# Delta rule mixer: projections in the order k, q, z, v, blocks sent ahead of a tile's wait, values solved and read out by halves of the heads

## The chip, the cores and the metric

The kernel runs on one core of one Trainium2 chip. The metric is the device time of one launch in microseconds (us), as the median of several runs. Engines: PE is TensorE (matmul), PEld its weight load, DVE VectorE, ACT ScalarE, SP the engine that issues the DMAs. GpSimd has nothing to do here.

## The reference, cut to what matters

The whole program is a chain of two stacks on an activation of 256 tokens x 1024. The first stack has two layers: a SwiGLU, a mixer, cross attention, a SwiGLU. The second has four layers of other mixers and MLPs. Everything is float32. The change touches one mixer, that of the second layer of the first stack, `deltanet_mixer`:

```python
qkv, z, a, b = jnp.split(h @ w_in, [3 * W, 4 * W, 4 * W + DN_HEADS], axis=-1)   # W = 1024, 8 heads of 128
qkv = jax.nn.silu(causal_dwconv(qkv, conv_w))                                  # 4 taps
q, k, v = jnp.split(qkv, 3, axis=-1)
q, k = l2norm(q), l2norm(k)
beta = sigmoid(b); g = -exp(a_log) * softplus(a + dt_bias)
# per head and chunk:
decay = exp(where(tril, gcum_i - gcum_j, -inf))
amat = eye + where(strict, (k*beta) k^T * decay, 0)
sol = triangular_solve(amat, [v*beta, k*beta*exp(gcum)], lower, unit_diagonal)  # u and w
qk = q k^T * decay
v_new = u - w @ state;  o = (q*exp(g)) @ state + qk @ v_new
state = state*exp(g_last) + (k*exp(g_last - g))^T @ v_new
o = rmsnorm(o, o_norm) * silu(z)
return o @ w_out
```

The result is added to the activation, and cross attention follows, whose keys and values are projections of another input, `mem`, that doesn't depend on the mixer.

## The kernel before, in words

**Weights.** All weight matrices lie in DRAM as 836 tiles of 128 x 1024 float32 (512 KB). Each is used once. For tile t, SP issues its DMA into one of three buffers SL (L2643) once VectorE has split tile t-3. ScalarE copies it to WH in a rounded format (`hi`, L1888), VectorE subtracts, WL = SL - WH (`lo`, L890), and TensorE multiplies with both halves. There are four buffers of WH and of WL: `hi(t)` waits until TensorE is through with tile t-4. A tile is four *blocks* of 128 x 256, and a block is six matmuls (two halves of the columns, each WH with the high part of the activation, WH with its low part, WL with the high part). `walk` on ScalarE and VectorE issues `hi` and `lo` of the tile three ahead at the start of each tile, then the engine's other work of that tile in the order of the code. So whatever stands ahead of a `hi` or a `lo` in its engine's stream delays it, and what waits for something slow delays all tiles after it.

**The stage.** The four projections of the mixer are the tiles 258 to 289, that is 128 blocks, numbered x = 0 to 127 in the order dn.k, dn.z, dn.q, dn.v (32 each, a group of 256 output columns every 8). After them come four small stages whose weights do not depend on the mixer: xv1a and xv1b (values for cross attention, 4 tiles each, 8 steps k of two blocks), xk1a and xk1b (its keys, 4 tiles each, 16 blocks), and then the mixer's output projection dn.o. The mixer's own arithmetic runs *beside* these blocks. Each engine has a function `beside(x)` that lists by block number what is to be issued ahead of block x. Nothing is scheduled at run time: the block numbers are the schedule, and each engine runs its stream in order.

**What runs beside** (TensorE's part in small float32 matmuls into three PSUM banks, taken in turn by `small`: the fourth use waits until the first was read):
- `taken(g)`, `taps(g)`, `conv(g)`, `gate(g)`: group g of k (0 to 3), q (4 to 7) or v (8 to 11) is evacuated on VectorE, its last tap is set on ScalarE, three taps are added on VectorE (six instructions), and SiLU is taken on ScalarE, for k and q with the squares.
- `squares(j)`: sums of squares over a head on TensorE; `spread` evacuates them. `log_sd` and `exp_sd` (ScalarE) turn four of them into the inverse norm, and `normalize` (VectorE) applies it. `log_sd` begins with a load of an activation table.
- `masked`, `exp_decay`: the decay matrices DC and its transpose DT, from the cumulated gates; `dkk`: k k^T per head, times DC; `dlt` its transpose.
- The 16 x 16 blocks on the diagonal of that matrix go through DRAM (`blocks_of_16` on SP) into a layout in which VectorE inverts them all at once (`eliminate`, 15 steps of two instructions), and back in two times eight DMAs into Y and YT.
- `invert`: three levels that double the size of the inverted blocks. In a level TensorE first makes four products dm, then four pairs dy and dyt; VectorE masks or subtracts each.
- `dkq`: k q^T, times DT; `dkt` and `keys`: k turned and scaled; `dvt` and `values`: v turned and scaled; `duu` and `dwt`: the solved values and keys; `dkv`: the state after the first chunk; `dws` with `less_state`; `do`: the output (`read_out`), evacuated by `output`. A number behind a name is a quarter q: two of a head's chunks times four heads; quarters 0 and 1 are the first chunk of the heads 0 to 3 and 4 to 7, 2 and 3 the second.
- `head_sums`, `sd_of`, `inverse_root`, `finish`, `finished`: the norm of the output, times silu(z), split into high and low parts for dn.o.

Of the kernel before, what the change touches and what calls it, by code (L numbers as in the profile page):

```python
# [49 lines left out]
def stage_table():  # L50
    rows = []
    for layer in range(2):
        rows += [(f"f1.{layer}.in", 8, 22, 1), (f"f1.{layer}.out", 22, 4, 1)]
        if layer == 0:
            rows += [("ab.q", 8, 2, 1), ("ab.k", 8, 2, 1), ("ab.x", 8, 2, 1), ("ab.v", 8, 1, 2), ("xk0", 8, 4, 1),
                     ("ab.g", 8, 2, 1), ("xv0", 8, 2, 2), ("ab.o", 8, 4, 1)]
        else:
            rows += [("dn.k", 8, 4, 1), ("dn.z", 8, 4, 1), ("dn.q", 8, 4, 1), ("dn.v", 8, 4, 1), ("xv1a", 8, 1, 2), ("xv1b", 8, 1, 2), ("xk1a", 8, 2, 1),
                     ("xk1b", 8, 2, 1), ("dn.o", 8, 4, 1)]
# [50 lines left out]
def build_program(nc, w, pk, cp, xT_in, mem_in, pos_in, out):  # L110
# [13 lines left out]
    with ctx:  # L124
# [90 lines left out]
        SUMMED = (33, 35, 37, 41, 84, 92, 100, 108)  # L215
# [42 lines left out]
        def tensor_program(p):  # L258
# [232 lines left out]
            def deltanet():  # L491
# [61 lines left out]
                def beside(x):  # L553
# [9 lines left out]
                    if 50 <= x < 54:  # L563
                        p.wait_ge(dn_qk.sem, dn_qk["k"])
                        four(("dkk", x - 50), lambda i: part(2048, 4 * (x - 50) + i), lambda i: part(2048, 4 * (x - 50) + i))
                    if 55 <= x < 59:
                        freed(("dkk", x - 55))
                        turned(("dlt", x - 55), lambda i: sl(L, x - 55, i))
                    if 88 <= x < 112:
                        invert((x - 88) // 8, (x - 88) % 8)  # L570
                    if 113 <= x < 117:
                        turned(("dkt", x - 113), lambda i: part(2048, 4 * (x - 113) + i))
                    if 122 <= x < 126:
                        p.wait_ge(dn_qk.sem, dn_qk["q"])
                        four(("dkq", x - 122), lambda i: part(2048, 4 * (x - 122) + i), lambda i: part(0, 4 * (x - 122) + i))
# [39 lines left out]
                for name in ("dn.k", "dn.z", "dn.q", "dn.v"):  # L615
# [3 lines left out]
                for j, k in gemm("xv1a", R67, R67, 0, 2048):  # L619
                    if k % 2 == 0:  # L620
                        p.wait_ge(mp_lo.sem, mp_lo[1, k // 2])
                    if k < 2:
                        solve_keys(2 + k)
                    if 3 <= k < 7:
                        q = (0, 2, 1, 3)[k - 3]
                        p.wait_ge(dn_act.sem, dn_act[9 + 2 * (q % 2)])
                        turned(("dvt", q), lambda i: part(4096, 4 * q + i))
                    if k == 5:
                        solve_values(0)
                    if k == 7:  # L630
                        solve_values(1)
                for j, k in gemm("xv1b", R67, R67, 0, 2048):
                    if k in (0, 1):
                        solve_values(2 + k)
                        add_keys(k)
                    if k in (2, 3):
                        read_out(k - 2)
                        less_state(k)
                    if k in (5, 6):
                        read_out(k - 3)  # L640
                for j, k in gemm("xk1a", R67, R67, 0, 2048):
                    if j == 0 and 1 <= k < 5:
                        head_sums(k - 1)
# [242 lines left out]
        def vector_program(v):  # L886
# [353 lines left out]
            def deltanet(gain):  # L1240
# [131 lines left out]
                def beside(x):  # L1372
# [15 lines left out]
                    if x in (24, 32) or x % 8 == 0 and x > 71:  # L1388
                        taken(x // 8 - (1 if x < 64 else 5))
                    if x in (25, 33) or x % 8 == 2 and x > 71:  # L1390
                        conv(x // 8 - (1 if x < 64 else 5))
# [4 lines left out]
                    if x in (35, 37, 40, 43):  # L1396
                        masked((35, 37, 40, 43).index(x))
                    if x % 8 == 7 and 32 <= x < 64:
                        scaled_to("dn.z", x // 8 - 4, BIG, 6144)
                    if x == 47:  # L1400
                        normalize("k", BIG[:, 2048:4096], PG[3], 1.0)
                    if 51 <= x < 55:
                        q = x - 51
# [4 lines left out]
                    if 66 <= x < 74:  # L1408
                        eliminate(2 * x - 132)
                        if x < 73:  # L1410
                            eliminate(2 * x - 131)
                    if x == 74:
                        own()
                        v.tensor_copy(TT, T.rearrange("p r c -> p c r")).then_inc(dn_sub.sem, dn_sub.give("t"))
                    if x == 87:
                        v.wait_ge(dn_exp.sem, dn_exp["er"])
                        v.tensor_copy(KE.unsqueeze(2), q4(DT)[:, :, 127:128]).then_inc(V.sem, V.up())
                    if 89 <= x < 113:
                        invert((x - 89) // 8, (x - 89) % 8)
                    if 114 <= x < 118:  # L1420
                        if x == 114:
                            own()
                            v.wait_ge(dn_beg.sem, dn_beg["g"])
                        keys(x - 114)
                    if x == 119:
                        normalize("q", BIG[:, 0:2048], PG[3], 128.0 ** -0.5)
                    if 123 <= x < 127:
                        q = x - 123
                        bk, free = had(("dkq", q))
                        v.tensor_tensor(QT[:, hc(q)], bk[:, :], DT[:, hc(q)], ALU.mult).then_inc(free, 1)  # L1430
                    if x == 127:
                        taken(11)
                        v.tensor_tensor(Q3, Q3, q4(ER[:, 1024:2048]), ALU.mult).then_inc(dn_qg.sem, dn_qg.give("qg"))
                    if x in (124, 126):
                        mem_low(x - 124)
                        mem_low(x - 123)
                for x in range(2):
                    v.memset(xp[x][:, :, 0:3], 0.0).then_inc(V.sem, V.up())
                x = 0
                for name in ("dn.k", "dn.z", "dn.q", "dn.v"):  # L1440
# [3 lines left out]
                for c in range(4, 8):  # L1444
                    mem_low(c)
# [1380 lines left out]
```

## Time and profile before

| | us |
|---|---|
| runs: median (lowest to highest of 3) | 2885.52 (2877.37 to 2886.12) |
| the profiled execution: device time | 2886.11 |
| its span in the trace | 2884.3 |
| PE busy | 2724.6 (94%) |
| DVE busy | 1819.3 (63%) |
| ACT busy | 1410.9 (49%) |
| mean granted clock of TensorE | 0.975 of full |

The span begins with the first instruction and ends with the last; the execution's own time is 1.8 us longer. Engines run beside each other, so busy times don't add up. A row of idle time gives in brackets how long an engine stood before the instruction and what released it. The granted clock is the share of full speed (2.4 GHz) that the throttle gave TensorE, 0.50 being 1.2 GHz.

### The profile page before, as it was taken

To read this page: it belongs to the slowest core of one execution; us is meant where nothing else is said; L and a number is where in the kernel's file an instruction comes from. 1 tells how busy PE (TensorE), PEld (TensorE's weight loads), DVE (VectorE), ACT (ScalarE), POOL (GpSimd) and SP (SyncE) were. 2 spreads that over 40 slices of the span, in tenths; PEclk is the share of its full clock that TensorE was granted. 3 is DMA by queue.
4 is the path that set the end of the run, shared out by engine and by line. 5 is a ranking of instruction groups with operands and counts; after the bars stand their busy time and mean duration, and the time that the engine had idled before them with its cause. 6 is when DMAs were issued, how large, how long until landed. Compare 5 with 4: busy or idle time off the path is not lost. (4 is left out here: it accounts for less than half of the span.)

```text
span 2884.3 us, 48970 instructions
## 1 busy us (share of the span) xinstructions
PE 2724.6 (94%) x21046; PEld 2631.0 (91%) x21046; DVE 1819.3 (63%) x2346; ACT 1410.9 (49%) x1924; POOL 0.2 (0%) x4
## 2 busy tenths in 40 slices
PE   7998989999998898999999999979999899999998
PEld 7998889999997878999888999979988899889998
DVE  5657656656656646666655765877554785655764
ACT  5445545454456354544445455544455544445443
POOL 0000000000000000000000000000000000000000
PEclk9999999999999999999999999999999999999999
DMA  6553435555543124455444455325542465444463
GB/s 211 176 190 126 162 109 194 183 190 184 189 146 114 59 96 146 162 187 190 159 153 134 154 198 162 109 66 191 193 154 95 143 198 190 152 163 137 154 196 128
DMA packets 129000, 450.09 MB, mean 156 GB/s; under 512 B 20112, under 2 KB 20368, under 8 KB 128528
## 3 DMA queue, kind: packets, MB, share of 16 engines
q1 hardware_dynamic: 128784, 446.96, 47.2%
q8 instruction: 166, 2.72, 0.4%
q14 instruction: 50, 0.41, 0.0%
HBM read 445.47 MB, written 1.44 MB: 155 GB/s over the span
## 5 line engine op out<-in xcount | busy, mean ns | idle before, releaser
L260 PE MATMUL B<-R,WH 128*128 128x256 f32 x10432 | 2105.4, 284 | 61.9 <-DVE R L956 37.1
L260 PEld LDWEIGHTS B<-R,WH 128*128 128x128 f32 x10432 | 1695.1, 191 | 76.6 <-DVE R L956 27.5
L890 DVE TENSOR_TENSOR WL<-SL,WH 128x1024 fp32r<-128x1024 f32 x836 | 1011.3, 1223 | 796.4 <-ACT WH L1888 795.4
L260 PE MATMUL B<-R,WL 128*128 128x256 f32 x4480 | 1267.1, 283 | 0.0
L1888 ACT ACTIVATE WH<-SL 128x1024 fp32r<-128x1024 f32 x836 | 866.4, 1053 | 576.3 <-PE B L260 475.8
L260 PEld LDWEIGHTS B<-R,WL 128*128 128x128 f32 x4480 | 857.3, 191 | 0.0
L260 PE MATMUL B<-RB,WH 128*128 128x256 f32 x1984 | 556.4, 280 | 0.0
L260 PE MATMUL B<-RB,WL 128*128 128x256 f32 x1728 | 482.5, 279 | 0.0
L260 PEld LDWEIGHTS B<-RB,WH 128*128 128x128 f32 x1984 | 373.6, 188 | 0.4 <-DVE WL L890 0.2
L260 PEld LDWEIGHTS B<-RB,WL 128*128 128x128 f32 x1728 | 324.0, 187 | 0.0
L260 PE MATMUL B<-WH,R 128*128 128x512 f32 x480 | 159.6, 402 | 3.1 <-DVE WL L890 3.0
L260 PE MATMUL B<-PG 128*128 128x256 f32 (+6 forms) x672 | 134.9, 349 | 12.1 <-DVE PG L1345 4.3
L260 PEld LDWEIGHTS B<-PG 128*128 128x128 f32 (+2 forms) x672 | 111.7, 197 | 27.6 <-issue 7.3
L1956 ACT ACTIVATE R<-X,PK 128x256 fp32r<-128x256 f32 x128 | 61.3, 505 | 118.5 <-DVE X L964 66.4
L2363 ACT ACTIVATE RB<-PG 128x512 fp32r<-128x512 f32 x64 | 40.5, 633 | 159.6 <-DVE PG L1484 159.6
L260 PEld LDWEIGHTS B<-WH,R 128*128 128x128 f32 x480 | 90.6, 189 | 28.8 <-DVE WL L890 5.2
L260 PE MATMUL B<-WL,R 128*128 128x512 f32 x240 | 95.2, 397 | 0.0
L260 PE MATMUL B<-PG,ONES 128*128 128x256 f32 (+1 forms) x242 | 71.6, 417 | 23.8 <-DVE PG L931 8.6
L2053 ACT ACTIVATE RB<-PG 128x512 fp32r<-128x512 f32 x44 | 27.8, 632 | 130.2 <-DVE PG L1048 130.2
L956 DVE SCALAR_TENSOR_TENSOR R<-X,PK,R 128x256 fp32r<-128x256 f32 x128 | 59.0, 483 | 29.1 <-ACT R L1956 29.1
L979 DVE TENSOR_TENSOR R<-PG,RB 128x512 fp32r<-128x512 f32 x108 | 73.9, 684 | 3.3 <-ACT RB L2053 2.8
L2050 ACT ACTIVATE PG<-PG 128x512 f32<-128x512 f32 x44 | 27.9, 633 | 91.7 <-DVE PG L1041 91.7
(280 smaller groups left out, 1522.5 us busy)
## 6 DMA issues: line engine op xcount, KB each, us to landing
SL<-in_w SPq DMA_DIRECT2D x836, 512.0 KB, 3.5
CP<-in_cp SPq DMA_DIRECT2D x5, 768.0 KB, 4.9
X<-in_xT SPq DMA_DIRECT2D x2, 512.0 KB, 6.6
PG<-in_mem SPq DMA_DIRECT2D x1, 1024.0 KB, 10.8
out<-X SPq DMA_DIRECT2D x1, 1024.0 KB, 3.9
PK<-in_pk SPq DMA_DIRECT2D x1, 594.5 KB, 3.8
dn_y<-PG SPq DMA_DIRECT2D x1, 256.0 KB, 4.1
PG<-dn_y SPq DMA_DIRECT2D x16, 16.0 KB, 2.0
```

Of the source, the lines that this page charges most:

```text
L260: return p.matmul(o, left, right, start=first, stop=final, skip_group_check=True)
L890: v.tensor_tensor(WL[t % NSPL][:, :], SL[t % NRAW][:, :], WH[t % NSPL][:, :].bitcast(F32), ALU.subtract).then_inc(s_lo, 1)
L956: v.scalar_tensor_tensor(R67[:, 2048 + c * 256:2304 + c * 256], X[:, cc(c)], gain(c), R67[:, cc(c)].bitcast(F32), ALU.mult, ALU.subtract). ...
L979: v.tensor_tensor(R03[:, hc(u)], d, RB[:, hc(u)].bitcast(F32), ALU.subtract).then_inc(hid_lo.sem, hid_lo.give((f, u)))
L1888: a.activation(WH[t % NSPL][:, :], SL[t % NRAW][:, :], ACT.Copy).then_inc(s_hi, 1)
L1956: a.activation(R67[:, cc(c)], X[:, cc(c)], ACT.Copy, scale=gain(c)).then_inc(h_hi.sem, h_hi.give((n, c)))
L2050: a.activation(s, s, ACT.Silu).then_inc(silu.sem, silu.give((f, u)))
L2053: a.activation(RB[:, hc(u)], PG[10][:, u % 4 * 512:u % 4 * 512 + 512], ACT.Copy).then_inc(hid_hi.sem, hid_hi.give((f, u)))
L2363: a.activation(RB[:, hc(x)], PG[10][:, x % 4 * 512:x % 4 * 512 + 512], ACT.Copy).then_inc(hid_hi.sem, hid_hi.give((f, x)))
```

## The change

Four things are changed, all in the schedule; no instruction's arithmetic is.

1. The projections run in the order k, q, z, v, and the weights are laid out in that order. So q's groups are convolved beside blocks 40 to 65, where z's groups were only evacuated, and `dkq` moves from block 122 to 84.
2. On SP, the DMAs of `blocks_of_16` stand ahead of the wait for the split of tile t-3, one tile number later.
3. The block numbers of the rest are moved to suit: `normalize("k")` from 47 to 50, `dkk` from 50 to 53, `eliminate` from 66 to 70, `invert` from 88 to 92, z's evacuation from 39 to 71 and on.
4. Behind the projections, quarters 0 and 2 (heads 0 to 3) are turned, solved and read out first, then 1 and 3, and the norm of the output follows earlier.

The core of the diff (of the table of weights and of what is only renumbered, a line or two):

```diff
-            rows += [("dn.k", 8, 4, 1), ("dn.z", 8, 4, 1), ("dn.q", 8, 4, 1), ("dn.v", 8, 4, 1), ...
+            rows += [("dn.k", 8, 4, 1), ("dn.q", 8, 4, 1), ("dn.z", 8, 4, 1), ("dn.v", 8, 4, 1), ...
-        SUMMED = (33, 35, 37, 41, 84, 92, 100, 108)
+        SUMMED = (24, 27, 38, 43, 57, 59, 66, 75)
 # TensorE
-                    if 50 <= x < 54:
+                    if 53 <= x < 57:                      # dkk
-                    if 55 <= x < 59:
+                    if x in (58, 60, 61, 62):             # dlt
+                    if 84 <= x < 88:                      # dkq, was 122 <= x < 126
-                    if 88 <= x < 112:
+                    if 92 <= x < 116:                     # invert
+                    if 116 <= x < 120:                    # dkt, was 113
+                    if x in (122, 124):
+                        solve_keys(x // 2 - 59)
+                    if x in (125, 127):
+                        turn_values(x - 125)
 # TensorE, xv1a
-                    if k < 2:
-                        solve_keys(2 + k)
...
+                    if k in (0, 2):
+                        solve_values(k)
+                    if k == 3:
+                        add_keys(0)
+                    if k in (4, 5):
+                        turn_values(2 * k - 7)
                     if k == 5:
-                        solve_values(0)
+                        less_state(2)
+                    if k == 6:
+                        solve_values(1)
+                        read_out(0)
                     if k == 7:
-                        solve_values(1)
+                        solve_values(3)
 # VectorE
+                    if x % 8 == 0 and (16 < x < 72 or x > 96):
+                        taken(x // 8 - (1 if x < 72 else 5))
+                    if x % 8 == (1 if x < 72 else 2) and (20 < x < 72 or x > 99):
+                        conv(x // 8 - (1 if x < 72 else 5))
-                    if x in (35, 37, 40, 43):
+                    if x in (35, 37, 67, 69):             # masked
-                    if x % 8 == 7 and 32 <= x < 64:
+                    if x % 8 == 7 and 64 <= x < 96:       # evacuation of z
-                    if x == 47:
+                    if x == 50:
                         normalize("k", BIG[:, 2048:4096], PG[3], 1.0)
-                    if 66 <= x < 74:
+                    if 70 <= x < 78:                      # eliminate
+                    if x == 82:
+                        normalize("q", BIG[:, 0:2048], PG[3], 128.0 ** -0.5)
+                    if x == 126:
+                        values(0)
 # VectorE, xv1a and xk1a
+                    if k == 0:
+                        conv(11)
+                        values(2)
+                    if k == 5:
+                        values(1)
+                    if k == 6:
+                        less_state(2)
+                        values(3)
-                    if j == 1 and k in (1, 5):
-                        finish(k // 2)
+                    if j == 0 and k in (4, 7):
+                        finish(k // 7 * 2)
 # ScalarE
-                    if x in (17, 22, 30, 37, 79, 87, 95, 102, 110, 118, 126):
+                    if x in (17, 22, 34, 38, 52, 53, 61, 70, 109, 117, 126):   # gate
-                    if x in (43, 111):
-                        log_sd(x // 111)
+                    if x in (45, 77):
+                        log_sd(x // 77)
-                        exp_decay("dc", DC, GC2, x - 46)
+                        exp_decay("dc", DC, GC2, x - 47)
+                    if 79 <= x < 83:
+                        exp_decay("dt", DT, NGC, x - 79)
-                    if (j, k) in ((0, 6), (1, 0)):
-                        finish(2 * j)
+                    if j == 0 and k in (1, 3):
+                        finish(k - 1)
 # SP
-                if t == T0 + 20:
+                if t == T0 + 21:                          # and each of the others one later
+                blocks_of_16(t)
                 if t >= NRAW:
                     s.wait_ge(s_lo, t - NRAW + 1)
-                blocks_of_16(t)
                 s.dma_start(SL[t % NRAW][:, :], w[t]).then_inc(s_w[t % NRAW], 16)
```

Where the change moves instructions, at three places. First VectorE around `normalize("k")` (the SCALAR_TENSOR_TENSOR of 128x2048), ahead of which TensorE waits for `dkk`. L890 is the split of a weight tile, L1263 `taken`, L1275 `conv`, L983 the evacuation of z, L1310 `masked` for DT, L1407 the product with DC. Before:

```order
L890 TENSOR_TENSOR WL<-SL,WH 128x1024
L1310 TENSOR_TENSOR PG<-CP,PG 128x1024 x2
L890 TENSOR_TENSOR WL<-SL,WH 128x1024
L983 TENSOR_TENSOR BIG<-B,RST 128x512
L1298 SCALAR_TENSOR_TENSOR BIG<-BIG,PG 128x2048
L890 TENSOR_TENSOR WL<-SL,WH 128x1024
L1407 TENSOR_TENSOR H<-B,PG 128x512
```

After (L906 is the split, L1279 `taken`, L1291 `conv`, L1314 `normalize`, L1423 the product with DC):

```order
L906 TENSOR_TENSOR WL<-SL,WH 128x1024
L1279 TENSOR_TENSOR PG<-B,RST 128x2x256
L1291 SCALAR_TENSOR_TENSOR BIG<-PG,PK,BIG 128x256 x6
L906 TENSOR_TENSOR WL<-SL,WH 128x1024 x2
L1279 TENSOR_TENSOR PG<-B,RST 128x2x256
L1291 SCALAR_TENSOR_TENSOR BIG<-PG,PK,BIG 128x256 x6
L1314 SCALAR_TENSOR_TENSOR BIG<-BIG,PG 128x2048
L906 TENSOR_TENSOR WL<-SL,WH 128x1024
L1423 TENSOR_TENSOR H<-B,PG 128x512 x2
```

The fourth and fifth groups (q's first two) are now evacuated and convolved ahead of the normalization of k, and so are two more splits.

Next ScalarE at the same place. Before: L1888 is `hi`, L2208 `spread`, L2214 and L2218 `log_sd` and `exp_sd`, L2224 `exp_decay`:

```order
L1888 ACTIVATE WH<-SL 128x1024
L2208 ACTIVATE PG<-B 128x512
L1924 ACT_TABLE_LOAD
L2214 ACTIVATE PG<-PG,PK 128x2048
L1888 ACTIVATE WH<-SL 128x1024
L2218 ACTIVATE PG<-PG 128x2048
L2275 ACTIVATE RT<-RT 128x16
L2277 ACTIVATE RT<-RT 128x16
L2224 ACTIVATE PG<-PG,RT 128x128 x8
L1888 ACTIVATE WH<-SL 128x1024
```

After: L1917 is `hi`, L2221 `taps`, L2237 `spread`, L2243 and L2247 `log_sd` and `exp_sd`, L2253 `exp_decay`:

```order
L1917 ACTIVATE WH<-SL 128x1024
L2221 ACTIVATE BIG<-PG,PK 128x256 x2
L1917 ACTIVATE WH<-SL 128x1024
L2237 ACTIVATE PG<-B 128x512
L1953 ACT_TABLE_LOAD
L2243 ACTIVATE PG<-PG,PK 128x2048
L2247 ACTIVATE PG<-PG 128x2048
L2313 ACTIVATE RT<-RT 128x16
L2315 ACTIVATE RT<-RT 128x16
L2253 ACTIVATE PG<-PG,RT 128x128 x4
L1917 ACTIVATE WH<-SL 128x1024
L2221 ACTIVATE BIG<-PG,PK 128x256 x2
L2253 ACTIVATE PG<-PG,RT 128x128 x12
```

The two `taps` of q came in, the `hi` between logarithm and exponential went, and a `hi` with a quarter of the decay matrix now stands between the exponential and the rest.

Last, VectorE in xk1a, where the output of the mixer is scaled (L1460, after L1489) and split into its low part (L1071, after L1087), four quarters in two calls of `finish`. Before:

```order
L1238 TENSOR_TENSOR BIG<-BIG 128x512 x4
L890 TENSOR_TENSOR WL<-SL,WH 128x1024 x2
L1460 SCALAR_TENSOR_TENSOR BIG<-BIG,PK,PG 128x256 x2
L1071 TENSOR_TENSOR R<-BIG,R 128x512
L1460 SCALAR_TENSOR_TENSOR BIG<-BIG,PK,PG 128x256 x2
L1071 TENSOR_TENSOR R<-BIG,R 128x512
L890 TENSOR_TENSOR WL<-SL,WH 128x1024
L1460 SCALAR_TENSOR_TENSOR BIG<-BIG,PK,PG 128x256 x2
L1071 TENSOR_TENSOR R<-BIG,R 128x512
L1460 SCALAR_TENSOR_TENSOR BIG<-BIG,PK,PG 128x256 x2
L1071 TENSOR_TENSOR R<-BIG,R 128x512
L890 TENSOR_TENSOR WL<-SL,WH 128x1024 x6
```

After:

```order
L906 TENSOR_TENSOR WL<-SL,WH 128x1024
L1254 TENSOR_TENSOR BIG<-BIG 128x512 x2
L906 TENSOR_TENSOR WL<-SL,WH 128x1024
L1489 SCALAR_TENSOR_TENSOR BIG<-BIG,PK,PG 128x256 x2
L1087 TENSOR_TENSOR R<-BIG,R 128x512
L1489 SCALAR_TENSOR_TENSOR BIG<-BIG,PK,PG 128x256 x2
L1087 TENSOR_TENSOR R<-BIG,R 128x512
L1489 SCALAR_TENSOR_TENSOR BIG<-BIG,PK,PG 128x256 x2
L1087 TENSOR_TENSOR R<-BIG,R 128x512
L1489 SCALAR_TENSOR_TENSOR BIG<-BIG,PK,PG 128x256 x2
L1087 TENSOR_TENSOR R<-BIG,R 128x512
L906 TENSOR_TENSOR WL<-SL,WH 128x1024 x8
```

Of the three splits ahead of and between the two calls of `finish`, two now stand behind both.

## Rows read from the trace of the kernel before

**Rows 1.** By window: PE, PEld, DVE, ACT, POOL busy us, clock, DMA, GB/s

```profile
845.00:926.00 81.00, 64.45 (x476) 60.01 (x475) 53.53 (x98) 55.65 (x96) 0.00 (x0) 0.92 0.35 107
926.00:988.00 62.00, 54.33 (x408) 51.99 (x409) 34.75 (x58) 15.56 (x21) 0.00 (x0) 0.92 0.23 70
988.00:1012.00 24.00, 19.48 (x155) 18.84 (x154) 21.10 (x34) 11.88 (x16) 0.00 (x0) 0.93 0.27 89
1012.00:1057.00 45.00, 39.53 (x233) 33.92 (x232) 19.39 (x27) 20.21 (x33) 0.00 (x0) 0.96 0.26 88
1057.00:1088.00 31.00, 28.21 (x205) 26.09 (x204) 17.40 (x24) 20.84 (x28) 0.00 (x0) 0.94 0.34 111
```

**Rows 2.** Timeline of TensorE, rows after a wait: start, us, work, [idle before, releaser]

```profile
853.75 1.13 PE L260 MATMUL B<-CP,PG 128*128 128x128 f32 x8 [1.62 <-ACT RT L2263]
...
879.68 1.65 PE L260 MATMUL B<-BIG 128*128 128x128 f32 x6 [2.73 <-DVE BIG L1298]
...
916.44 2.05 PE L260 MATMUL B<-PG,ONES 128*128 128x512 f32 x2 [5.80 <-ACT PG L2204]
...
926.01 1.25 PE L260 MATMUL B<-PG 128*128 128x128 f32 x8 [3.93 <-issue]
...
950.41 0.85 PE L260 MATMUL B<-PG 128*128 128x128 f32 x4 [2.16 <-DVE PG L1345]
...
1083.14 0.51 PE L260 MATMUL B<-R,WH 128*128 128x256 f32 x2 [2.79 <-DVE WL L890]
```

**Rows 3.** By window: the clock after a short and a longer wait

```profile
937.30:941.30 4.00, 3.99 (x35) 4.00 (x36) 1.52 (x3) 0.00 (x0) 0.00 (x0) 1.00 0.43 135
951.00:954.00 3.00, 3.00 (x16) 3.00 (x15) 3.00 (x8) 0.00 (x0) 0.00 (x0) 0.50 0.23 90
```

**Rows 4.** Timeline of VectorE: the pace of tiles, undisturbed

```profile
816.53 1.23 DVE L890 TENSOR_TENSOR WL<-SL,WH 128x1024 fp32r<-128x1024 f32 x1 [1.60 <-ACT WH L1888]
819.36 1.23 DVE L890 TENSOR_TENSOR WL<-SL,WH 128x1024 fp32r<-128x1024 f32 x1 [1.60 <-ACT WH L1888]
```

**Rows 5.** Timeline of TensorE: two groups of four products, a block between

```profile
882.71 1.05 PE L260 MATMUL B<-BIG 128*128 128x128 f32 x8
...
884.31 0.94 PE L260 MATMUL B<-BIG 128*128 128x128 f32 x7
```

**Rows 6.** Timeline of ScalarE around log_sd

```profile
870.63 0.60 ACT L2208 ACTIVATE PG<-B 128x512 f32<-128x512 f32 x1 [0.45 <-PE B L260]
871.25 1.28 ACT L1924 ACT_TABLE_LOAD   x1
872.55 2.01 ACT L2214 ACTIVATE PG<-PG,PK 128x2048 f32<-128x2048 f32 x1
...
875.40 1.90 ACT L2218 ACTIVATE PG<-PG 128x2048 f32<-128x2048 f32 x1
...
877.42 2.43 ACT L2224 ACTIVATE PG<-PG,RT 128x128 f32<-128x128 f32 x8
```

**Rows 7.** Timeline of VectorE: taken, conv, normalize

```profile
860.52 0.68 DVE L1263 TENSOR_TENSOR PG<-B,RST 128x512 f32<-128x512 f32 x1
862.25 2.47 DVE L1275 SCALAR_TENSOR_TENSOR BIG<-PG,PK,BIG 128x256 f32<-128x256 f32 x6 [1.04 <-ACT BIG L2192]
...
877.34 2.29 DVE L1298 SCALAR_TENSOR_TENSOR BIG<-BIG,PG 128x2048 f32<-128x2048 f32 x1
```

**Rows 8.** Groups of VectorE, 901 to 913 us: the elimination

```profile
L1329 DVE TENSOR_TENSOR PG<-PG 128x15 f32<-128x15 f32 (+7 forms) x15 | 3.1, 208 | 0.5
```

**Rows 9.** Timeline of SP: the blocks on their way through DRAM

```profile
916.41 0.33 SPq L2624 DMA_DIRECT2D dn_y<-PG  x1
...
920.54 3.86 SPq L2629 DMA_DIRECT2D PG<-dn_y  x8
```

**Rows 10.** Timeline of VectorE: finish, one quarter and the next

```profile
1070.34 0.87 DVE L1460 SCALAR_TENSOR_TENSOR BIG<-BIG,PK,PG 128x256 f32<-128x256 f32 x2
...
1072.52 0.88 DVE L1460 SCALAR_TENSOR_TENSOR BIG<-BIG,PK,PG 128x256 f32<-128x256 f32 x2
```

More of the change, by code:

```diff
@@ L57, in stage_table @@
         else:
-            rows += [("dn.k", 8, 4, 1), ("dn.z", 8, 4, 1), ("dn.q", 8, 4, 1), ("dn.v", 8, 4, 1), ("xv1a", 8, 1, 2), ("xv1b", 8, 1, 2), ("xk1a", 8, 2, 1),
+            rows += [("dn.k", 8, 4, 1), ("dn.q", 8, 4, 1), ("dn.z", 8, 4, 1), ("dn.v", 8, 4, 1), ("xv1a", 8, 1, 2), ("xv1b", 8, 1, 2), ("xk1a", 8, 2, 1),
                      ("xk1b", 8, 2, 1), ("dn.o", 8, 4, 1)]
@@ new lines, in beside @@
+                    if 85 <= x < 89:
+                        q = x - 85
+                        if q == 0:
+                            v.wait_ge(dn_exp.sem, dn_exp["er"])
+                            v.tensor_copy(KE.unsqueeze(2), q4(DT)[:, :, 127:128]).then_inc(V.sem, V.up())
+                            own()
+                        bk, free = had(("dkq", q))
+                        v.tensor_tensor(QT[:, hc(q)], bk[:, :], DT[:, hc(q)], ALU.mult).then_inc(free, 1)
+                    if x == 90:
+                        v.tensor_tensor(Q3, Q3, q4(ER[:, 1024:2048]), ALU.mult).then_inc(dn_qg.sem, dn_qg.give("qg"))
@@ L1422, in beside @@
+                    if 93 <= x < 117:
+                        invert((x - 93) // 8, (x - 93) % 8)
+                    if 117 <= x < 121:
+                        if x == 117:
                             own()
                             v.wait_ge(dn_beg.sem, dn_beg["g"])
[L1424 to L1430, printed above, removed]
@@ L1431, in beside @@
-                    if x == 127:
-                        taken(11)
-                        v.tensor_tensor(Q3, Q3, q4(ER[:, 1024:2048]), ALU.mult).then_inc(dn_qg.sem, dn_qg.give("qg"))
+                        keys(x - 117)
                     if x in (124, 126):
@@ L1436, in beside @@
                         mem_low(x - 123)
+                    if x == 126:
+                        values(0)
+                    if x == 127:
+                        taken(11)
                 for x in range(2):
@@ L1448, in deltanet @@
                         conv(11)
-                    if k > 3:
-                        values((0, 2, 1, 3)[k - 4])
-                for j, k in walk("xv1b"):
-                    if k in (3, 4):
-                        less_state(k - 1)
+                        values(2)
[4 more added lines that the diff above has]
+                        values(3)
+                for j, k in walk("xv1b"):
+                    if k == 3:
+                        less_state(3)
+                    if k == 6:
+                        turn_on(0)
+                        turn_on(1)
                 def finish(j0):
```

186 lines of the change are left out of this document (96 added, 90 removed).

## The prediction

> **What bounds the kernel now.** The page first: TensorE is busy for 2724.6 us of 2884.3, so only its idle time and its slow time can be won. The windows next, over the stretch that the change touches [rows 1]: TensorE stands idle for 16.6, 7.7, 4.5, 5.5 and 2.8 us (width less busy), 37.1 us in all. The projections up to block 84 and the blocks' way through DRAM lie in the first, the inversion in the second, the turned keys and `dkq` in the third, values and read-out in the fourth, xk1a and xk1b in the fifth. Then TensorE's timeline, for what each wait was for [rows 2]: 2.73 before `dkk` for the normalization of k; 5.80 before the first sum of squares of q, whose convolution stood behind the elimination on VectorE; 3.93 before the inversion, with no engine named: the blocks on their way back from DRAM; 2.16 between two levels of the inversion; 2.79 in xk1b, for the split of a weight tile.
>
> A wait costs more than itself. After the wait of 2.16 the clock stands at 0.50, which is 1.2 GHz; after one of 1.3 it stays at 1.00, 2.4 GHz [rows 3]; after the 1.62 [rows 2] it stays too. The missing clock in the five windows is 6.5, 5.0, 1.7, 1.8 and 1.9 us, 16.9 together; the stretch has nine waits of over 2 us (five of them in rows 2), so 1.8 us each.
>
> **Units.** A tile of four blocks takes 2.83 us [rows 4], a block 0.71. Two groups of four products with a block between start 1.60 apart [rows 5], so a group costs 0.89; a sum of squares has as many columns, and I take the same 0.85 to 0.9, a turned group half. VectorE's split costs 1.2 [rows 4], `taken` 0.65, `conv` 2.45, and between them 1.04 for ScalarE's `taps`; `normalize` 2.3 [rows 7]. On ScalarE a small evacuation costs 0.6, the table load 1.3, logarithm 2.0, exponential 1.9, a quarter of a decay matrix 1.2 (half of the 2.43) [rows 6]; I take `hi` at 1.05, the distance from the logarithm's end to the exponential's start being 0.84 to one `hi`. The elimination is 15 steps of two instructions of 0.21, with gaps 0.47 a step [rows 8]: 7 us.
>
> **Blocks 24 to 84.** TensorE now asks for sums of squares at 24 and 27, ahead of ScalarE: I count 1.1, 0.7 and, before the first product of the gates (its PSUM bank is now freed by a `spread`), 1.9, then 1.0 at 38. In return the 2.49 that was there goes, since `gate(2)` no longer stands before the evacuations, and so does the 1.62. So TensorE ends block 31 at 859.0 and `taken(3)` starts at 861.2, against 860.52 [rows 7].
> The path to `dkk` from there: on VectorE `taken`, 1.0 for the taps, `conv`, two `masked` of 1.2, two splits and `taken(4)`, together 9.6, to 870.8. On ScalarE taps 0.9, `hi` 1.05, `spread` 0.6, table load, logarithm, exponential 5.2, two tiny ones 0.2, a quarter of DC 1.2, `hi` 1.05: 10.2, to 881.0. Back on VectorE split 1.2, `taken(5)` 0.65, taps 1.0, `conv(5)` 2.45, `normalize` 2.3: 7.6, to 888.6. TensorE has 21 blocks, one group, two sums of squares and the wait of 1.0 to do from 859.0 and is at block 53 at 877.5. So the wait before `dkk` is 11.2 instead of 2.73. This is what q in z's place costs: z was one evacuation, q is a convolution ahead of the normalization.
> The Trainium skill (ScalarE: Activation LUTs, What ACT_TABLE_LOAD costs) puts a switch of tables at 1.28 us and 1.38 more for a drain. Here the logarithm starts 0.02 us after the load of 1.28 has ended [rows 6], so the row decides; by the page this wait would be 1.4 us longer.
> Behind it, VectorE reads the third and fourth `dkk` only after `hi` and split of their tile, `taken(6)` and `conv(6)`; the bank of the fourth is asked for at block 59. That is waits of 0.35 and 2.45.
> The path to `dkq` at 84, from the end of block 63: `hi` 1.05, split, `taken(7)`, taps, `conv(7)` 5.3, two `masked` and a split 3.6, then elimination 7, two evacuations of z 1.3, three more splits 3.5, the copy 0.4, `normalize("q")` 2.3: 24.5, and 24.7 with the hops between engines. TensorE takes 15.9 for 20 blocks and two sums. That is a wait of 8.8 in place of the 5.80, so VectorE's queue, not the DMA, decides.
> Sum of the stretch: 4.7 + 11.2 + 2.8 + 8.8 = 27.5, against 16.6, in which the 3.93 lies.
>
> **The blocks through DRAM.** The transfer out took 4.1 us to be seen and the eight back 3.9 to issue and about 1.6 to land [rows 9], 9.6 from the elimination's copy. In the new order the copy ends 4.1 us before `dkq` may start, and TensorE then has four groups, eight blocks and slow clock, 11 us. The Y blocks land 5.5 us early, the YT blocks too. So the 3.93 goes, and of the DMA order itself I cost nothing: the tile behind it is needed about two tiles later. Bounds for that: none, or all of the 3.93 back.
>
> **Inversion.** No group of q is convolved in it but two of v are, no sum of squares stands between, and the first boundary of a level has no `taken`. A boundary then costs `hi`, split and one subtraction, 2.9, less a group and a block, 1.6: 1.3 and not 2.16. I count 0.4, 1.3, 1.05, 0.8, 1.2, 0.3: 5.1 against 7.7, and no fall of the clock. Keys and `dkq`: `conv(9)` no longer stands before `keys(0)` and `dkq` has gone: 0.5 against 4.5.
>
> **Values and read-out.** `solve_values(0)` waits 1.5 for `values(0)`, which stands behind two `mem_low`. `solve_values(2)` at step 2 waits for `values(2)` behind `conv(11)`: that starts about 7 us after the last block of v, and TensorE is there after 5.3: 4.8. `read_out(0)` takes the bank of `dvt3`, freed by `values(3)` behind `hi`, split and `less_state(2)`, 3.5 after a block that TensorE leaves 0.9 before: 2.6. Together 8.9 against 5.5.
>
> **xk1a.** One quarter of `finish` takes 2.2 [rows 10], the two calls 8.7. Before, a split stood between them. Now the split of the second tile of xk1b stands behind both. From the stage's start ScalarE has two evacuations, a `hi`, three sums, the table load, two logarithms and exponentials of half width and a `hi`: 10.5; split 1.2; then 8.7 and 1.2: 21.6 to 22. TensorE wants that tile after 15.9. A wait of 6.1 against 2.8.
>
> **Sum.** 27.5 + 5.1 + 0.5 + 8.9 + 6.1 = 48.1 us of waits against 37.1: 11.0 more. Waits over 2 us: six (11.2, 2.45, 8.8, 4.8, 2.6, 6.1) against nine: 3 x 1.8 = 5.4 less. Net 5.6 us: 2886.1 (the profiled execution, 0.6 over the median of the runs) + 5.6 = 2891.7, so 2891 for a median. No more than no change: a measurement here tells 0.3%, 8.7 us, which is 2877 to 2894.
>
> **Rivals.**
> (a) *The short waits lower the clock as well; slower.* Seven of the new waits lie between 1.0 and 1.9 us: two of them stand within 8 us (1.1 and 1.9, with 0.7 between), three in the inversion. The row of 1.62 speaks against, the one of 2.16 for a point near it. If four of them bring a fall: + 7.2, 2899. It decides from a point under 1.5 us.
> (b) *The two long waits don't form; faster.* If ScalarE and VectorE reach `normalize` in time for blocks 53 and 84, each wait is at most 1.9: 9.3 + 6.9 less, and two falls of 1.8: 19.8 less, 2872. For it: VectorE is busy for 53.5 of 81 us and ScalarE for 55.7 [rows 1], so there is room if their orders fit. Against: the chains above hold hardly a gap.
> (c) *The last wait doesn't form*, because `finish` starts a whole tile earlier than I count: 6.1 + 1.8 less, 2884. For it: the norm's sums start two blocks of xv1b earlier. Against: both calls ahead of the split.
> (d) That sending the blocks early does nothing is in the forecast already: they are early because TensorE is late.
>
> **How the numbers follow.** Forecast 0.45 (own range 2884 to 2899; of it 0.32 no change, 0.10 slower, 0.03 faster), (a) 0.17, slower; (b) 0.15, faster; (c) 0.23, of it 0.20 no change and 0.03 slower. So faster 0.18, same 0.52, slower 0.30. The range takes in (c), (a) and part of (b): 2875 to 2901.
>
> **What would show it.** Right: a wait of about 11 before `dkk` released by `normalize`, about 9 before `dkq` released by the same line, no wait named issue before the inversion, no half clock inside the inversion, a wait of about 6 for the split behind `finish`. Wrong: a wait before `dkk` under 5; sums of waits in the stretch far from 48; a change of time from outside the tiles 258 to 306.

## The result, and the profile after

| us | before | after |
|---|---|---|
| median of the runs | 2885.52 (2875.13 to 2889.63, 7 runs) | 2896.12 (2892.03 to 2898.96, 7 runs) |
| ratio | | 1.0043, 95% interval 1.0026 to 1.0061 |
| profiled execution, its span | 2886.11, 2884.3 | 2896.12, 2894.3 |
| PE, DVE, ACT busy | 2724.6, 1819.3, 1410.9 | 2724.4, 1817.4, 1411.2 |
| mean granted clock | 0.975 | 0.974 |

The changed kernel is slower by 0.43%: the two medians are 10.6 us apart, and the ratio, with its interval, stands for 12 us (7.5 to 17.6). 2891 was forecast, as no change. The engines do the same work in the same busy time. What grew is TensorE's idle time in the stretch that the change touches. The windows of the profile after, over the same parts of the program as [rows 1] (busy us by engine, clock, DMA share, GB/s):

```profile
845.00:934.00 89.00, 63.64 (x458) 57.99 (x458) 57.26 (x107) 62.42 (x104) 0.00 (x0) 0.90 0.31 99
934.00:944.70 10.70, 10.68 (x81) 10.68 (x82) 5.33 (x8) 1.78 (x2) 0.00 (x0) 0.86 0.46 90
944.70:998.00 53.30, 47.38 (x403) 45.95 (x402) 34.01 (x54) 12.16 (x17) 0.00 (x0) 1.00 0.21 70
998.00:1009.00 11.00, 10.49 (x87) 10.08 (x88) 9.13 (x15) 5.06 (x8) 0.00 (x0) 1.00 0.30 98
1009.00:1059.00 50.00, 41.20 (x231) 35.74 (x230) 20.51 (x32) 20.16 (x34) 0.00 (x0) 0.90 0.23 81
1059.00:1096.00 37.00, 31.29 (x214) 28.97 (x213) 19.11 (x25) 22.73 (x29) 0.00 (x0) 0.91 0.35 118
```

In the order of the program: projections up to `dkq`, `dkq`, inversion, turned keys, values and read-out, xk1a and xk1b. The first is idle for 25.4 us where the first of [rows 1] had 16.6; the inversion for 5.9 at a clock of 1.00 where it had 7.7 at 0.92; values and read-out for 8.8 instead of 5.5, the last for 5.7 instead of 2.8. TensorE's rows after the longest waits, which answer to [rows 2]:

```profile
888.27 2.08 PE L260 MATMUL B<-BIG 128*128 128x128 f32 x8 [10.57 <-DVE BIG L1314]
...
902.49 1.85 PE L260 MATMUL B<-PG,ONES 128*128 128x512 f32 x2 [2.09 <-DVE H L1423]
...
934.02 2.07 PE L260 MATMUL B<-BIG 128*128 128x128 f32 x8 [8.08 <-DVE BIG L1314]
...
1021.95 1.80 PE L260 MATMUL B<-PG 128*128 128x128 f32 x8 [4.39 <-DVE PG L1372]
...
1036.69 2.05 PE L260 MATMUL B<-PG 128*128 128x128 f32 x8 [2.86 <-DVE PG L1372]
...
1085.01 0.79 PE L260 MATMUL B<-R,WH 128*128 128x256 f32 x2 [5.71 <-DVE WL L906]
```

L1314 is `normalize`, L1423 the product with DC, L1372 `values`, L906 the split. All waits of 0.3 us or more from block 24 to xk1b add up to 46.6 us (before: 37.0). Of the 9.6 us more, 3.4 lie up to the turned keys and 6.2 behind them. The clock in four of the places behind them:

```profile
882.20:892.20 10.00, 3.93 (x18) 3.93 (x19) 6.80 (x10) 9.05 (x20) 0.00 (x0) 0.50 0.32 105
929.90:936.70 6.80, 2.68 (x12) 2.68 (x13) 5.88 (x7) 4.82 (x12) 0.00 (x0) 0.51 0.67 195
1022.20:1025.60 3.40, 3.40 (x13) 3.00 (x13) 0.63 (x1) 0.60 (x1) 0.00 (x0) 0.50 0.46 159
1083.40:1090.20 6.80, 5.19 (x24) 5.19 (x25) 4.83 (x5) 3.62 (x5) 0.00 (x0) 0.52 0.56 185
```

In three of the four the half clock (1.2 GHz) began while TensorE still stood idle and went on over the work after the wait; in the third it began 0.3 us after the work had (at 1022.2, the wait ended at 1021.95). I add up TensorE's busy time at half clock from 844.9 to 1125 us. Half of it is what the clock costs, since at full clock it would take half as long. Before: nine falls, 29.7 us of slow work, 14.9 us lost. After: six falls, 25.4 us of slow work, 12.7 lost. So the stretch takes 9.6 us more in waits and, by this count, 2.1 less in clock. Up to the last instruction of the mixer's sum (at 1111.83 before, 1120.25 after) it ended 8.4 us later. That is 9.6 us of waits less 1.2 us of TensorE's busy time; why busy time fell by 1.2 and not by 2.1 is open. The two spans are 10.0 us apart.

### The profile page after: what moved, and what is told of

The parts are those of the page before. It is cut to its first block and busy times, and to the rows that moved or that the text cites. A ratio compares the mean times of both kernels' runs of the same rounds, so it can differ in the third digit from the quotient of the medians.

```text
span 2894.3 us, 48968 instructions
## 1 busy us (share of the span) xinstructions
PE 2724.4 (94%) x21046; PEld 2628.7 (91%) x21046; DVE 1817.4 (63%) x2346; ACT 1411.2 (49%) x1924; POOL 0.2 (0%) x4
## 5 line engine op out<-in xcount | busy, mean ns | idle before, releaser
L906 DVE TENSOR_TENSOR WL<-SL,WH 128x1024 fp32r<-128x1024 f32 x836 | 1010.8, 1223 | 801.9 <-ACT WH L1917 800.9
L1917 ACT ACTIVATE WH<-SL 128x1024 fp32r<-128x1024 f32 x836 | 866.2, 1053 | 581.9 <-PE B L260 471.1
L260 PE MATMUL B<-PG 128*128 128x256 f32 (+6 forms) x672 | 135.9, 350 | 14.5 <-DVE PG L1372 8.8
L260 PEld LDWEIGHTS B<-PG 128*128 128x128 f32 (+2 forms) x672 | 112.0, 197 | 30.9 <-issue 11.2
## 6 DMA issues: line engine op xcount, KB each, us to landing
PG<-in_mem SPq DMA_DIRECT2D x1, 1024.0 KB, 10.6
```

Source lines behind the costliest of these rows:

```text
L260: return p.matmul(o, left, right, start=first, stop=final, skip_group_check=True)
L906: v.tensor_tensor(WL[t % NSPL][:, :], SL[t % NRAW][:, :], WH[t % NSPL][:, :].bitcast(F32), ALU.subtract).then_inc(s_lo, 1)
L1917: a.activation(WH[t % NSPL][:, :], SL[t % NRAW][:, :], ACT.Copy).then_inc(s_hi, 1)
```

## Experiments

"Waits" are those of TensorE in the stretch, "loss" is half of its slow work there, both of one profiled execution; medians and ratios are over all runs. "Distance" is from the first product of the gates' wide sums (853.89 in the changed kernel) to the last instruction of the mixer's sum, 266.4 us there. A median says what a kernel takes; waits, loss and distance say what happened in a single run. The kernel before had medians of 2884.78 in the runs of the first four, 2885.01 in those of the next four and 2886.31 in the last three.

**1. The kernel before, with the DMAs ahead of the wait alone.**

```diff
-                if t >= NRAW:
-                    s.wait_ge(s_lo, t - NRAW + 1)
                 blocks_of_16(t)
+                if t >= NRAW:
+                    s.wait_ge(s_lo, t - NRAW + 1)
```

> The kernel before with one part of the change: on SP the block DMAs stand ahead of the wait for the split, at the same tile numbers. Theory (the order of projections and of the tail makes the loss, the DMA order makes nothing): the transfer out starts at the end of the elimination's copy instead of 1.2 us later behind a split, so the wait before the inversion (3.93 in the kernel before) becomes about 2.8 and the kernel 1.1 us faster, which no timing can tell from none. Rival (the DMAs ahead of a weight tile starve the split): a wait of ScalarE for DMA or a wait of TensorE for WL appears in the stretch, several us slower.

Measured: 2881.93, ratio 0.9986 (0.9972 to 1.0). TensorE at the start of the inversion:

```profile
926.30 1.13 PE L260 MATMUL B<-PG 128*128 128x128 f32 x8 [0.94 <-issue]
```

The 3.93 of [rows 2] has become 0.94, 3.0 us less, where the theory had 1.1; the medians differ by 2.9, at the edge of what the interval can tell from nothing. SP's rows:

```profile
918.51 0.33 SPq L2624 DMA_DIRECT2D dn_y<-PG  x1
...
920.52 3.77 SPq L2629 DMA_DIRECT2D PG<-dn_y  x8
```

The transfer out starts at the end of the elimination's copy; in the kernel before it started 1.2 us after it, as the theory said. The rest is that it was seen 2.0 us later and not 4.1 [rows 9]. That part isn't shown to come from the DMAs' place: in experiment 2 the weight tile follows the transfer as closely as in the kernel before (0.37 us), and there it took 2.3. So the place is worth 1.2 us surely and at most 3. No DMA starved a split: the rival fell.

**2. The changed kernel, with SP's order and tile numbers of before** (the same lines of the diff, turned round).

> The changed kernel with the DMA order and the tile numbers of before. Theory: the blocks are early by more than 5 us, so no wait before the inversion appears and the stretch stays within 0.5 us of the changed kernel. Rival (sending ahead of the wait is what removed the 3.93): a wait of 1 to 4 us comes back before the inversion and the kernel is 2 to 6 us slower than the changed one.

Measured: 2896.36, 1.0033 (1.0018 to 1.0048). Every wait is within 0.05 us of the changed kernel's, and no wait named issue appears. In the new order the DMAs' place is worth nothing.

**3. The changed kernel, `normalize("k")` at 47.**

```diff
-                    if x == 50:
+                    if x == 47:
                         normalize("k", BIG[:, 2048:4096], PG[3], 1.0)
```

> The changed kernel with the normalization of k at block 47 again, so ahead of two convolutions' worth of VectorE work (one split, taken, conv) instead of behind it. Theory of a chain (ScalarE and VectorE together are the bound of blocks 32 to 60): the wait before dkk falls from 10.6 to about 2.8, but waits of about 2.5, 3 and 2.4 appear for gate(4), the third and the fourth dkk, so TensorE reaches block 64 only 2.5 to 3 us earlier. Rival (the wait is one misplaced instruction): TensorE is 7 to 8 us earlier at block 64 and the kernel 8 us faster than the changed one.

Measured: 2889.31, 1.0018 (1.0006 to 1.0031). Its rows of TensorE:

```profile
882.30 1.16 PE L260 MATMUL B<-BIG 128*128 128x128 f32 x8 [3.00 <-DVE BIG L1314]
...
891.51 1.83 PE L260 MATMUL B<-BIG 128*128 128x128 f32 x7 [4.14 <-DVE H L1423]
...
900.25 1.12 PE L260 MATMUL B<-PG,ONES 128*128 128x512 f32 x2 [1.31 <-DVE H L1423]
```

Three waits with 8.4 us stand for three with 13.3, and the rest is unchanged. The distance is 5.8 shorter, between the 2.5 to 3 of the theory and the 7 to 8 of the rival. What stood ahead of the normalization shows on VectorE, in the changed kernel and then here (L1917 is `hi`, L2247 the exponential):

```profile
880.68 1.23 DVE L906 TENSOR_TENSOR WL<-SL,WH 128x1024 fp32r<-128x1024 f32 x1 [5.35 <-ACT WH L1917]
...
885.94 2.28 DVE L1314 SCALAR_TENSOR_TENSOR BIG<-BIG,PG 128x2048 f32<-128x2048 f32 x1
```

```profile
879.95 2.29 DVE L1314 SCALAR_TENSOR_TENSOR BIG<-BIG,PG 128x2048 f32<-128x2048 f32 x1 [3.03 <-ACT PG L2247]
```

Here the normalization starts as soon as the exponential has ended. In the changed kernel it starts 7.6 us after it: 2.3 for ScalarE's quarter of a decay matrix and `hi`, 5.3 for VectorE's split, `taken`, the taps between, and the convolution. Of the 7.6, 2.8 come back behind it, where the banks of `dkk` are read no earlier.

**4. The changed kernel, behind the projections as before** (the order of solving, reading out and `finish` restored).

> The changed kernel with everything behind the projections as before (turning, solving, reading out, norm and finish), the projections as changed. Theory: the waits of the tail fall from 14.5 us to about 8.3 and slow TensorE work from 14.9 us to 6.8, so 6.2 + 4.1 = 10 us faster than the changed kernel, about 2886, equal to the kernel before. Rival (the loss lies in the projections): no more than 3 us faster, since waits of the turned values and keys that the projections now hid come back.

Measured: 2889.03, 1.0015 (1.0004 to 1.0026). Rows:

```profile
1008.46 1.86 PE L260 MATMUL B<-PG 128*128 128x128 f32 x7 [2.86 <-DVE R L1372]
...
1079.72 0.57 PE L260 MATMUL B<-R,WH 128*128 128x256 f32 x2 [2.79 <-DVE WL L895]
```

The waits behind the projections are 9.75 us instead of 14.5, the loss 8.5 instead of 12.7, the distance 8.4 shorter. So the larger part of what the change costs is the new order behind the projections, not that of the projections: 1.8 us of waits in solving and reading out by halves, 2.9 in the wait for the split behind `finish`. The rival's no more than 3 us is refuted, but the kernel isn't equal to the kernel before either, as I expected.

**5. `finish(2)` later, at block 12 of xk1a instead of 7.** On ScalarE `finished(2)` moves with it.

```diff
-                    if j == 0 and k in (4, 7):
-                        finish(k // 7 * 2)
+                    if k == 4:
+                        finish(2 * j)
```

> The changed kernel with the second call of finish three splits later on VectorE (at block 12 of xk1a instead of 7), and ScalarE's part of it to match. Theory (the wait of 5.7 for a weight tile in xk1b is made of the two calls standing ahead of one split): it becomes two waits of about 1.8 and 1.0, 2.9 us less, at most one fall of the clock there instead of one or two. Rival (the late inverse norm on ScalarE makes that wait): it stays above 5.

Measured: 2896.31, 1.0036 (1.0022 to 1.005). The 5.71 became two:

```profile
1084.35 0.50 PE L260 MATMUL B<-R,WH 128*128 128x256 f32 x2 [1.70 <-DVE WL L906]
...
1092.31 0.66 PE L260 MATMUL B<-R,WH 128*128 128x256 f32 x2 [2.04 <-DVE WL L906]
```

2.0 us less waiting, 1.3 less distance (the loss was 13.0), and no difference in the medians. The second wait was 2.0 where I expected 1.0: in the trace two splits stand between the calls, at 1083.07 in one row of x2, and not three. So the third still stands behind both.

**6. `solve_values(2)` one step later, `add_keys(0)` too, `read_out(0)` behind `solve_values(3)`.**

```diff
-                    if k in (0, 2):
-                        solve_values(k)
-                    if k == 3:
+                    if k in (0, 3):
+                        solve_values(k // 3 * 2)
+                    if k == 4:
                         add_keys(0)
```

> The changed kernel with three calls on TensorE one step later: solve_values(2) and add_keys(0), and read_out(0) behind solve_values(3). Theory (what is waited for doesn't move; VectorE's conv(11) and values(3) set the times): the wait of 4.4 becomes 3.0, the wait of 2.9 becomes 1.2, 3.0 us less in all. Rival (the later calls only push the same waits into xv1b): the sum of the waits of both stages stays within 1 us of the 8.8 of the changed kernel.

Measured: 2891.26, 1.0011 (1.0 to 1.0023). Rows:

```profile
1026.57 1.23 PE L260 MATMUL B<-PG 128*128 128x128 f32 x8 [2.84 <-DVE PG L1372]
...
1039.89 2.02 PE L260 MATMUL B<-PG 128*128 128x128 f32 x16 [1.46 <-DVE PG L1372]
```

4.39 and 2.86 became 2.84 and 1.46; with one new wait of 0.48 that is 2.5 less, where the theory had 3.0. The loss is 10.3, the distance 4.5 shorter: in this one profile nearly half of what two steps in a stream gave was clock.

**7. `dkq` four blocks later.** VectorE's product with DT (85 to 88, now 89 to 92) and the scaling of q (90, now 95) move with it.

```diff
-                    if 84 <= x < 88:
+                    if 88 <= x < 92:
```

> The changed kernel with the products of k and q at blocks 88 to 91 instead of 84 to 87. Theory (VectorE's queue from the seventh convolution through the elimination to the normalization of q sets the moment): the wait of 8.1 becomes 5.2, and no wait appears before the inversion, since the Y blocks have landed about 2 us before. Rival (the time to the inversion is set by the blocks through DRAM): the 2.8 us come back as a wait with no engine named before the inversion.

Measured: 2897.62, 1.004 (1.0027 to 1.0053). Rows:

```profile
937.86 1.43 PE L260 MATMUL B<-BIG 128*128 128x128 f32 x5 [5.28 <-DVE BIG L1314]
...
955.39 1.16 PE L260 MATMUL B<-PG,H 128*128 128x128 f32 x8 [1.62 <-DVE H L1353]
```

Of 2.8 us taken from the wait 1.1 came back at the start of the inversion, released by VectorE and not by the DMAs; neither the theory (nothing comes back) nor the rival (all of it does, with no engine named) has this. The loss rose to 13.2: 1.0 less distance. The medians show none of it.

**8. The edits of 3, 5, 6 and 7 together.**

> The changed kernel with the three edits of these runs and the normalization of k at block 47. Theory (waits of different places add up): 46.6 us of waits less 4.8, 2.9, 3.0 and 2.8 is 33, against 37 in the kernel before, so about 4 us faster than before if the clock falls as often, 2881. Rival (each wait removed turns into one further on): waits stay above 40 and the kernel is not faster than before.

Measured: 2883.61, 0.9993 (0.9981 to 1.0004). The waits are 36.2 us. The four savings (4.8, 2.0, 2.5 and 1.7, together 11.0) nearly add up, to 10.4; the loss is 10.9, the distance 12.4 shorter, the median 12.5. The 2881 of the theory isn't reached, nor are waits above 40 as the rival has it. The changed order can do without most of its long waits, and then it is level with the kernel before.

**9. The changed kernel, with TensorE kept at work in four waits.**

```diff
+                def warm(count):
+                    n = len(took)
+                    b = 4 + n % 3
+                    p.wait_ge(s_bank[b], n // 3)
+                    for i in range(count):
+                        mm(BK[b][:, 0:128], ONES[:, :], ONES[:, :])
...
                     if 53 <= x < 57:
+                        if x == 53:
+                            warm(43)
                         p.wait_ge(dn_qk.sem, dn_qk["k"])
```

> The changed kernel with idle TensorE kept at work: ahead of four of its long waits (dkk, dkq, solve_values(2), the second tile of xk1b) 43, 32, 15 and 21 products of 128x128 whose result nobody reads and the next group overwrites. At 0.22 us each they take 9.6, 7.1, 3.3 and 4.7 us of waits of 10.57, 8.08, 4.39 and 5.71. Theory (the half clock follows the idle time and costs half of the work done in it): no half clock behind these four, whose slow work in the changed kernel was 4.25, 2.87, 3.42 and 5.48 us, so 8.0 us less: 2888. The wait of 2.09 and the one of 2.86 keep theirs. Rival 1 (the idle time has nothing to do with it): the falls stay where they were, 2896. Rival 2 (the products themselves run at half clock and end late): each wait is followed by up to as much again, 2900 or more.

Measured: 2887.19 (2880.76 to 2895.73, 12 runs), 1.0004 (0.9994 to 1.0014), where the changed kernel had 1.0026 to 1.0061. The waits' ends, and the windows that answer to those with half clock above:

```profile
891.84 1.16 PE L260 MATMUL B<-BIG 128*128 128x128 f32 x8 [0.97 <-DVE BIG L1329]
...
935.52 1.16 PE L260 MATMUL B<-BIG 128*128 128x128 f32 x8 [0.96 <-DVE BIG L1329]
...
1080.64 0.51 PE L260 MATMUL B<-R,WH 128*128 128x256 f32 x2 [1.02 <-DVE WL L921]
```

```profile
882.00:893.00 11.00, 10.03 (x90) 9.84 (x89) 7.63 (x10) 9.08 (x23) 0.00 (x0) 1.00 0.14 48
929.00:937.00 8.00, 7.04 (x63) 6.85 (x63) 7.04 (x12) 7.19 (x18) 0.00 (x0) 1.00 0.52 169
1020.00:1024.00 4.00, 3.11 (x23) 2.76 (x23) 3.01 (x6) 1.23 (x2) 0.00 (x0) 1.00 0.34 122
1078.00:1085.00 7.00, 5.98 (x52) 5.79 (x51) 4.16 (x5) 4.57 (x7) 0.00 (x0) 1.00 0.44 135
```

The normalization of k comes no sooner (TensorE goes on 34.4 us after the first wide product in both kernels), but the clock stays at 1.00. One fall is left, behind the wait of 2.08; the loss is 1.6 instead of 12.7, the distance 10.3 shorter. Both rivals fall. It isn't this one profile alone: the granted clock has a mean of 0.980 over these 12 runs and of 0.973 over the changed kernel's seven. The distance gave more than the 8.0 expected, since the fall behind the 2.86, whose wait I had not filled, did not come either; whether that was chance no run shows. So the four long waits of the changed kernel cost their 28.8 us and some 8 of clock, all its falls some 10.

**10. The same in all_four** (9, 19 and 9 products).

> The kernel with four moves (all_four) with such products ahead of dkk (9), dkq (19) and solve_values(2) (9), in waits of 2.99, 5.27 and 2.81 us. Theory: the slow work behind the last two (6.22 and 3.42 us) goes, 4.8 us less than all_four: 2879; behind dkk the waits of 2.57 and 1.93 keep their falls. Rival (the clock has nothing to do with the idle time): as all_four, 2884.

Measured: 2884.54, 0.9991 (0.9981 to 1.0001). One fall, loss 3.0 against 10.9, distance 6.2 shorter. The profiled execution took 2878.11, the shortest of its eleven, but the median is not under that of experiment 8, and the 2879 of the theory isn't reached. The mean clock did rise, from 0.9765 to 0.9780. Why no time came of it is open.

**11. The same in sp_alone** (8, 21, 10 and 8).

> The kernel before with the blocks sent ahead (sp_alone) and such products in the waits of 2.73 (dkk, 8 products), 5.80 (first sum of squares of q, 21), 3.25 (first turned quarter of v, 10) and 2.79 (fourth tile of xk1b, 8). Theory: of sp_alone's falls those of 3.73 and 5.94 us slow work go, 4.8 us less: 2877, which would be the fastest of all kernels here, 0.3% under the kernel before; those that the kernel before had behind dkk and behind the wait of 3.25 cannot come either. Rival: as sp_alone, 2882.

Measured: 2881.05, 0.9984 (0.9974 to 0.9994): the fastest median here, under the kernel before by 0.16%, but no better than experiment 1. TensorE got to the inversion sooner and met the blocks on their way:

```profile
917.05 1.10 PE L260 MATMUL B<-PG,ONES 128*128 128x512 f32 x2 [1.13 <-ACT PG L2219]
923.53 1.13 PE L260 MATMUL B<-PG 128*128 128x128 f32 x8 [2.56 <-issue]
```

2.56 and not 0.94: counted from the first wide product TensorE got there 0.9 us sooner than in experiment 1, and the blocks landed 0.7 later. What the clock gave there went to the wait for DRAM. And a fall that sp_alone's profile doesn't have came behind 2.48. The loss is 6.5 against 9.1, the distance only 0.4 shorter. The 2877 expected isn't reached.

## Why the prediction was wrong in one term and right in the rest

- **Blocks 24 to 53.** Forecast 4.7 and 11.2; measured 4.4 (1.06, 0.49, 1.72, 1.12) and 10.57, released by `normalize`. The cause holds: experiment 3. Of ScalarE's path the load and logarithm read here

```profile
873.08 1.28 ACT L1953 ACT_TABLE_LOAD   x1
874.37 2.01 ACT L2243 ACTIVATE PG<-PG,PK 128x2048 f32<-128x2048 f32 x1
```

  with 0.01 between, as in [rows 6]. The Trainium skill (ScalarE: Activation LUTs, What ACT_TABLE_LOAD costs) adds 1.38 us for a drain; neither trace shows it.
- **Banks of `dkk`, `dkq`.** Forecast 2.8 and 8.8; measured 2.7 (0.59, 2.09) and 8.08. So VectorE's queue decides, not the DMA: experiment 2 leaves the 8.08 as it was, and experiment 7 shortens it by the 2.8 that four blocks take.
- **The blocks through DRAM.** Forecast: the 3.93 goes, the DMAs' own place is worth nothing. Both hold (experiment 2). In the old order the place was worth 1.2 to 3 us (experiment 1). The 9.6 us "from the elimination's copy" count from the issue; from the copy's end at 915.25 it is 10.8, and the transfer out, taken as 4.1, took 2.6 after the change.
- **Inversion, keys.** Forecast 5.1 and 0.5, no fall; measured 5.9 and 0.51, the clock 1.00. A wait of 1.56 stands in it twice, one of 1.26 once, and outside it four more lie between 1.0 and 1.8; behind none of the seven does the clock fall. Rival (a), that short waits lower the clock, did not happen.
- **Values and read-out, xk1a.** Forecast 8.9 and 6.1; measured 8.8 and 5.71. Experiments 4 to 6 bear the causes out: moving `finish` or the three calls moves the waits. Rivals (b) and (c) had these waits not form; they formed.
- **The sum of waits.** 48.1 forecast, 46.6 measured: + 9.6 instead of + 11.0.
- **The clock is the step that failed.** I counted falls, nine to six, at 1.8 us each: 5.4 us back. The falls were six, but the loss went from 14.9 to 12.7, 2.1 back, and TensorE's busy time fell by 1.2. A price per fall was wrong: the half clock behind the 10.57 lasted 10.24 us, 4.24 of them busy, behind the last wait 6.83, 5.48 of them busy. Where the waits grow, fewer falls cost as much. The price was also taken from the clock missing in the windows, which counts half clock while TensorE stands idle and loses nothing (4.4 of 34.1 us before, 12.1 of 37.6 after). By that same measure the six windows above miss 18.7 us where those of [rows 1] miss 16.9: it rose, with three falls fewer. With 2.1 in place of 5.4 my own sum would have been 11.0 - 2.1 = 8.9 us, 0.31%, and the forecast slower. That term is what held the forecast inside no change.
- **Even the 2.1 is the difference of two single executions.** Of the nine waits of over 2 us in the kernel before, experiment 1 lacks only the 3.93, and its loss is 9.1, not 14.9; the changed kernel and experiments 2, 5 and 7 have 12.7 to 13.2. The granted clock of every run says more: its mean is 0.9749 over the 87 further runs of the kernel before, 0.9733 over the 19 of the changed kernel and of experiment 2, whose waits are the same. That is 72.5 and 77.2 us of missing clock, 4.7 more (standard error 0.9). In the stretch, by the two profiles, 3.9 us more of it fell on idle time. So, as an estimate from these numbers, the clock gave back nothing that stands clear of the noise.

2896 lies in the stated range, and in the 2884 to 2899 of the forecast, but above the 2894 up to which it called no change. The net was forecast at 5.6 us and came out at 10.6. It would have been further off had the waits not been forecast 1.4 us too large.

Little of the measured difference stays open. The 87 runs of the kernel before have a mean of 2885.5, the 19 of the changed kernel and experiment 2 one of 2895.4: 9.9 us, and 9.6 of waits with a clock that gave nothing back account for it. In the profiled executions it is 10.0, of which 8.4 by the end of the stretch and 1.6 after it. The unchanged rest of the program (0 to 845 and 1126 to 2870 us) lost 39.3 us to the clock in the profile before, 42.2 in the one after, and 47.4, 49.4 and 51.0 in those of experiments 2, 1 and 8, with the same work. One execution is therefore not enough to price falls there, and I can't say whether the 1.6 us belong to the changed kernel.

## What to carry to other kernels

Order two chains by what stands ahead of the instruction that is waited for, engine by engine: what was moved ahead of a normalization cost 7.6 us at its place, though 5 of them could be had back by one number. Price the clock by the work that runs slow behind each wait, not by the count of waits; a long wait can be filled with products that nobody reads. That gave 9 us in the changed kernel, with its waits of 4.4 to 10.6, and nothing in the medians of the two kernels with shorter ones (up to 5.8), in one of which TensorE next met a wait for a DMA. Before adopting an order that shortens one chain, look whether what it hides was worth its cost alone: here one part of the change was worth 1.2 to 3 us in the old order and nothing in the new.

## What the runs showed of the hardware that was not expected

- Most waits repeat to 0.05 us from one execution to the next (10.57, 10.56, 10.56 and 10.56 in the changed kernel and experiments 2, 4 and 5), but falls of the clock don't. Behind that wait the half clock lasted 10.24 us in these four kernels and 13.65 in those of experiments 6 and 7, whose code up to there is the same. Of the start of a kernel the Trainium skill (TensorE: Matmul & The Clock Gate, Part 1: The HAM clock gate) says that the moment at which the clock rises varies from run to run; the traces here show the like in the middle of one.
- Where the clock differs, waits can too: up to the products `dkk` experiments 3 and 8 have the same code, and among them the one waits once, 4.14, the other twice, 2.57 and 1.93.
- The loss in the unchanged part differs by 12 us between executions. It is not shown to make the spread of one kernel's runs (2875 to 2890 for the kernel before): over the 87 further runs of that kernel time and missing clock go together loosely (correlation 0.56), over the 12 of experiment 1 not at all (-0.13).
- In sp_alone's profile no fall came behind waits of 2.47, 2.73 and 3.33; in the profile before one of 2.16 had one [rows 2, 3].
- Forty-three products of 128 x 128 from one operand, back to back, took 9.8 us, 0.23 each, and TensorE's clock stayed at 1.00 over them.
